# A two-layer hybrid block on one core: set-up work moved at the turns of the stages, and the second layer's projections cut to the tokens that the output needs

## The reference, cut to what matters

```python
h = concatenate([meta, x], 1)                      # 528 tokens
h = h + ssd_retention_mixer(rmsnorm(h, g0), ...)   # layer 0
h = h + conv_ffn(rmsnorm(h, g1), ...)
h = h + sb_lru_mixer(rmsnorm(h, g2), ...)          # layer 1
h = h + conv_ffn(rmsnorm(h, g3), ...)
return rmsnorm(h, final_norm)[:, N_META:]          # N_META = 16

def conv_ffn(h, w_in, conv_w, conv_b, w_out):
    u = causal_dwconv(h @ w_in, conv_w, conv_b)    # 3 taps: a token and the two before it
    g, up = jnp.split(u, 2, -1)
    return (jax.nn.silu(g) * up) @ w_out

def sb_lru_mixer(h, ...):
    q, k, v, gate, xr = split_cols(h @ w_in, ...)
    y_sb = stick_breaking_attention(q, k, v)       # causal: queries see the keys before them
    y_lru = rg_lru(causal_dwconv(xr, ...), ...) * gelu(gate)   # a scan over the tokens
    return concatenate([y_sb, y_lru], -1) @ w_out
```

## Time and profile before

| | |
|---|---|
| median of 3 runs | 1885.35 us (1885.19 to 1885.55) |
| profiled execution | 1886.69 us |
| its span, first to last instruction | 1884.7 us |
| PE busy | 1825.9 us, 97% of the span |
| DVE busy | 1221.8 us, 65% |
| ACT busy | 755.5 us, 40% |
| POOL busy | 68.5 us, 4% |
| mean granted TensorE clock | 0.994 |

### The profile page before, as it was taken

The page is one execution under the profiler, slowest core; times in us unless marked ns, Lnnn a source line. Parts: engine busy times, 40 slices in busy tenths (PEclk is TensorE's granted clock), DMA queues, the critical chain, the costliest instruction groups (busy, mean ns, idle before and its releaser), DMA issues.

```text
span 1884.7 us, 36044 instructions
## 1 busy us (share of the span) xinstructions
PE 1825.9 (97%) x14286; PEld 1737.0 (92%) x14286; DVE 1221.8 (65%) x1740; ACT 755.5 (40%) x1135; POOL 68.5 (4%) x140
## 2 busy tenths in 40 slices
PE   7999999999999999999999999999899999999996
PEld 7999998999899999999998888888789999999996
DVE  7787756455456777774334777777775688878323
ACT  5444432121234222222224777777774422223221
POOL 0122220000000000000000000000000000000000
PEclk9999999999999999999999999999999999999998
DMA  4222213222222222232222111111112222223221
GB/s 150 91 80 79 90 49 111 68 68 67 68 71 86 89 89 89 89 97 95 90 78 72 58 59 49 59 58 59 57 45 79 89 89 89 89 89 102 93 92 60
DMA packets 39938, 149.92 MB, mean 80 GB/s; under 512 B 4384, under 2 KB 5408, under 8 KB 39216
## 3 DMA queue, kind: packets, MB, share of 16 engines
q1 hardware_dynamic: 38672, 142.16, 24.1%
q10 hardware_dynamic: 1184, 6.60, 1.0%
HBM read 146.62 MB, written 2.13 MB: 79 GB/s over the span
## 4 chain that ended last, share of the span: by engine, by line
PE 71%; issue 12%; DVE 9%; ACT 6%; POOL 2%; DMA 0%; DVEq 0%; ACTq 0%; POOLq 0%
PE gp L359 60%; PE small L403 3%; PE small L414 3%; DVE spb L1502 1%; DVE sp_lo L1524 1%; ACT lbuf L922 1%; DVE wlo L1059 1%; ACT lbuf L925 1%; PE small L576 1%; POOL dec L1664 1%; PE small L553 1%; ACT whi L661 1%; PE small L561 1%; ACT L927 1%; ACT L995 0%
## 5 line engine op out<-in xcount | busy, mean ns | idle before, releaser
L359 PE MATMUL gp<-hn_hi,whi 128*128 128x264 f32 x3216 | 664.6, 288 | 23.0 <-DVE wlo L1059 12.2
L359 PE MATMUL gp<-hn_hi,wlo 128*128 128x264 f32 x3216 | 657.4, 286 | 0.0
L359 PE MATMUL gp<-hn_lo,whi 128*128 128x264 f32 x3216 | 656.7, 286 | 0.0
L661 ACT ACTIVATE whi<-raw 128x1024 fp32r<-128x1024 f32 (+1 forms) x249 | 273.6, 1099 | 775.5 <-PE gp L359 774.5
L1059 DVE TENSOR_TENSOR wlo<-raw,whi 128x1024 fp32r<-128x1024 f32 (+1 forms) x249 | 317.5, 1275 | 390.1 <-ACT whi L661 389.6
L359 PEld LDWEIGHTS gp<-hn_hi,whi 128*128 128x128 f32 x3216 | 503.0, 189 | 29.2 <-DVE wlo L1059 14.2
L359 PEld LDWEIGHTS gp<-hn_hi,wlo 128*128 128x128 f32 x3216 | 500.7, 189 | 0.0
L359 PEld LDWEIGHTS gp<-hn_lo,whi 128*128 128x128 f32 x3216 | 500.3, 189 | 0.0
L359 PE MATMUL gp<-hid_hi,whi 128*128 128x264 f32 x704 | 142.6, 284 | 0.0
L359 PE MATMUL gp<-hid_lo,whi 128*128 128x264 f32 x704 | 142.5, 284 | 0.0
L359 PE MATMUL gp<-hid_hi,wlo 128*128 128x264 f32 x704 | 142.5, 283 | 0.0
(11 more groups left out here) (241 smaller groups left out, 1907.1 us busy)
## 6 DMA issues: line engine op xcount, KB each, us to landing
raw<-in SPq DMA_DIRECT2D x217, 512.0 KB, 3.6
raw<-in SPq DMA_DIRECT2D x32, 704.0 KB, 4.1
cs_bc<-cs_scratch ACTq DMA_DIRECT2D x4, 1056.0 KB, 6.2
hT<-in SPq DMA_DIRECT2D x4, 528.0 KB, 7.4
out<-yT SPq DMA_DIRECT2D x4, 512.0 KB, 2.8
rdec<-in ACTq DMA_DIRECT2D x1, 1056.0 KB, 8.9
gw<-in SPq DMA_DIRECT2D x8, 128.0 KB, 3.4
rope<-in ACTq DMA_DIRECT2D x1, 528.0 KB, 5.8
```

The costliest lines, as they stand in the source:

```text
L359: ins = pe.matmul(gp[t.par][:, h, 0:H2], wp[w.par][:, cols], rp[:, k0 + k, h * H2:(h + 1) * H2], start=first and k == 0 and n == 0, stop=l ...
L661: act.activation(whi[w.par][:, 0:kt * P], raw[w.par][:, 0:kt * P], ACT.Copy).then_inc(hi_done, 1)
```

## The change

In layer 1, queries and gates, the output projection and the feed-forward's first product are computed for tokens 12 and on (t0 = FROM_MIX1), the convolution and hidden state for 14 and on, the feed-forward's second product for 16 and on. Halves are of 258 and 256 tokens then. Keys, values and xr stay whole. `gemm`, `evacuate`, `conv` and `add_tile` take a first token t0; each unit keeps its number of matmuls. The first 12 columns of qs and gt are set to zero once.

At the turns: the sum of squares goes behind k tile 3; the late `y_part` has its weight split behind k == 5 in place of 3, with the evacuation of tile 7 just ahead of that split; the first rotation of the queries goes behind split_lo and tile 7; hb and nsp (with ACT's three operations) are prepared at the start of the kernel; the memsets ahead of layer 1 go to GpSimd (POOL), behind `nlo_done` = 24, and DVE waits for them (`zero_done`) ahead of the first attention block.

```diff
+FROM_MIX1, FROM_CONV1, FROM_OUT = 12, 14, N_META
@@ gemm
-                            ins = pe.matmul(gp[t.par][:, h, 0:H2], wp[w.par][:, cols],
-                                            rp[:, k0 + k, h * H2:(h + 1) * H2],
+                            ins = pe.matmul(gp[t.par][:, h, 0:half], wp[w.par][:, cols],
+                                            rp[:, k0 + k, t0 + h * half:t0 + (h + 1) * half],
@@ norm_behind
-                return lambda k: sum_squares(n) if k == 1 else None
+                return lambda k: sum_squares(n) if k == 3 else None
@@ TensorE, layer 1
+            def l1_from(c):
+                return FROM_MIX1 if c in (0, 3) else 0
-                hgemm(At(0, 0, W_OUT1 + c), At(0, 0, T_OUT1 + c), after=after)
+                hgemm(At(0, 0, W_OUT1 + c), At(0, 0, T_OUT1 + c), after=after, t0=FROM_MIX1)
-            project(W_OUT1 + KD, T_OUT1 + KD, y_hi, y_lo, KD, (ylo_done, 3 * KD), per=1)
-            ffn_in(W_FI1, T_FI1, 3)
-            project(W_FO1, T_FO1, hid_hi, hid_lo, KH, (hlo_done, KF))
+            project(W_OUT1 + KD, T_OUT1 + KD, y_hi, y_lo, KD, (ylo_done, 3 * KD), per=1, t0=FROM_MIX1)
+            ffn_in(W_FI1, T_FI1, 3, t0=FROM_MIX1)
+            project(W_FO1, T_FO1, hid_hi, hid_lo, KH, (hlo_done, KF), t0=FROM_OUT)
@@ ScalarE, start
+            ch.link(act.activation(nspt[:], pcol("lru_lam", 0, 8), ACT.Abs))
             act.wait_ge(dtx_done, 1)
             ch.link(act.activation(dtl, dtx, ACT.Abs))
+            act.activation(nspt[:], nspt[:], ACT.Exp, scale=-1.0)
             ch.link(act.activation(dtl, dtl, ACT.Exp, scale=-1.0))
             act.activation(dtl, dtl, ACT.Ln, bias=1.0).then_inc(dtl_done, 1)
+            act.activation(nspt[:], nspt[:], ACT.Ln, bias=1.0).then_inc(spl_ln, 1)
@@ ScalarE, y_part (both late halves with split_at=5)
-                    if k == 3:
+                    if k == split_at:
                         split_hi(At(0, 0, wb + 1))
@@ ScalarE, into layer 1
             act.wait_ge(spl_done, 1)
-            ch.link(act.activation(nspt[:], pcol("lru_lam", 0, 8), ACT.Abs))
-            ch.link(act.activation(nspt[:], nspt[:], ACT.Exp, scale=-1.0))
-            act.activation(nspt[:], nspt[:], ACT.Ln, bias=1.0).then_inc(spl_ln, 1)
-            act.wait_ge(spl_done, 2)
@@ VectorE, start (behind the scan of csr)
+                    ve.tensor_scalar(hb[:, 0, :], pcol("lru_ba", 0, 8), 0.5, None, ALU.mult)
+                    ve.tensor_scalar(hb[:, 1, :], pcol("lru_bx", 0, 8), 0.5, None, ALU.mult)
+                    ch.link(ve.tensor_scalar(nsp[:], pcol("lru_lam", 0, 8), -1.0, 0.0, ALU.mult, ALU.max))
+                    ve.wait_ge(spl_ln, 1)
+                    ch.link(ve.tensor_tensor(nsp[:], nsp[:], nspt[:], ALU.add))
+                    ve.tensor_scalar(nsp[:], nsp[:], -0.5 * LRU_C, None, ALU.mult).then_inc(spl_done, 1)
@@ VectorE, retention
                         ret_tile(r - 1, 7)
                         if isinstance(r, int) and r == 1:
+                            rotate(0, rq, qr, 1, ch.link)
                             ve.wait_ge(rot_done, 1)
                             rotate(0, rk, kr, 3, ch.link)
...
             ve.wait_ge(tab_in, 32)
-            rotate(0, rq, qr, 1, ch.link)
             ret_stage(1)
@@ VectorE, y_part
-                    if k == 3:
+                    if k == split_at:
+                        if between is not None:
+                            between()
                         split_lo(At(0, 0, wb + 1))
...
-            add_tile(At(0, 0, W_OUT0 + 7), At(0, 0, T_OUT0 + 7), 7)
-            y_part(y_hi, y_lo, LATE[0], W_OUT0 + KD, KD)
+            y_part(y_hi, y_lo, LATE[0], W_OUT0 + KD, KD, 5, lambda: add_tile(At(0, 0, W_OUT0 + 7), At(0, 0, T_OUT0 + 7), 7))
@@ VectorE, layer 1 (the memsets and the preparation behind invert(2) are gone)
+                t0 = FROM_MIX1 if c in (0, 3) else 0
+                evacuate(w, t, halves(dst, t0), SB_SCALE if c == 0 else None, t0=t0)
...
+            ve.wait_ge(zero_done, 1)
             for b in range(2):
                 l1_block(0, b)
@@ GpSimd, behind the retention stage
+            po.wait_ge(nlo_done, 3 * KD)
+            for s in range(2):
+                po.memset(qs[s][:, 0:FROM_MIX1], 0.0)
+            po.memset(gt[:, 0:FROM_MIX1], 0.0)
+            po.memset(ubx[:, 0:3], 0.0)
+            for gap in (slice(WJ[1], LATER1), slice(LATER1 + WJ[2], LATER2), slice(LATER2 + WJ[3], LATER3)):
+                po.memset(later[:, gap], 0.0)
+            po.memset(spb[:, FULL:CAUSAL], 0.0)
+            po.memset(sp_lo[:, FULL:CAUSAL].bitcast(f32), 0.0)
+            po.memset(sp_hi[:, FULL:CAUSAL].bitcast(f32), 0.0).then_inc(zero_done, 1)
```

More of the change, by code:

```diff
@@ L150, in build @@
         eps_col = sb("eps_col", [P, 1])
+        hb = sb("hb", [P, 2, 8])
+        nsp, nspt = sb("nsp", [P, 8]), sb("nspt", [P, 8])
         idle_g, idle_v, idle_a = (sb(n, [P, 6]) for n in ("idle_g", "idle_v", "idle_a"))
@@ L231, in build, with halves, gout @@
         sp_ = ctx.enter_context(nc.psum_tensor("small", [P, 4, 512], f32))
[L233 to L237, removed]
+        def halves(ap, t0=0):
+            return ap[:, t0:T].rearrange("p (h t) -> p h t", h=2)
+        def gout(s, t0=0):
+            return gp[s][:, :, 0:(T - t0) // 2]
         def pcol(name, c=0, n=1, rows=P):
@@ L282, in build @@
             sem(n) for n in ("sum_done", "sphi_done", "later_done", "lathi_done", "latlo_done"))
-        prep_done, spl_done, spl_ln = sem("prep_done"), sem("spl_done"), sem("spl_ln")
+        prep_done, spl_done, spl_ln, zero_done = sem("prep_done"), sem("spl_done"), sem("spl_ln"), sem("zero_done")
         block = ctx.enter_context(nc.Block())
@@ L347, in _, with gemm @@
         def _(pe):
-            def gemm(w, t, rhs_hi, rhs_lo, k0=0, kt=KD, first=True, last=True, ready=None, after=None):
+            def gemm(w, t, rhs_hi, rhs_lo, k0=0, kt=KD, first=True, last=True, ready=None, after=None, t0=0):
+                half = (T - t0) // 2
                 pe.wait_ge(lo_done, w.v + 1)
@@ L366, in gemm, with hgemm @@
                         after(k)
-            def hgemm(w, t, ready=None, after=None):
-                gemm(w, t, hn_hi, hn_lo, ready=ready, after=after)
+            def hgemm(w, t, ready=None, after=None, t0=0):
+                gemm(w, t, hn_hi, hn_lo, ready=ready, after=after, t0=t0)
             def sum_squares(n):
@@ L504, in _, with project @@
                 ret_small(RET_HEADS - 1, c)
-            def project(wb, tb, rhs_hi, rhs_lo, kt, ready, per=2):
+            def project(wb, tb, rhs_hi, rhs_lo, kt, ready, per=2, t0=0):
                 def tile(i, s, first_pair):
@@ L510, in tile @@
                         gemm(At(2 * per, i, wb + per * s + kh), At(2, i, tb + s), rhs_hi, rhs_lo, k0=kh * kt, kt=kt,
-                             first=kh == 0, last=kh == per - 1, ready=ready if first_pair and s == 0 else None)
+                             first=kh == 0, last=kh == per - 1, ready=ready if first_pair and s == 0 else None,
+                             t0=t0)
                 for s in range(2):
@@ L627, in l1_block @@
                     hgemm(At(10, i, W_L1 + 5 * (b + 1) + c), At(10, i, T_L1 + 5 * (b + 1) + c),
-                          ready=ready if c == 0 else None, after=after)
+                          ready=ready if c == 0 else None, after=after,
+                          t0=FROM_MIX1 if ready is not None else l1_from(c))
             for c in range(5):
                 hgemm(At(10, 0, W_L1 + c), At(10, 0, T_L1 + c), ready=(nlo_done, 2 * KD) if c == 0 else None,
-                      after=norm_behind(2) if c == 0 else None)
+                      after=norm_behind(2) if c == 0 else None, t0=l1_from(c))
             for b in range(2):
@@ L1375, in _, with y_part @@
             ch.leave(2, RET_HEADS)
-            def y_part(dst_hi, dst_lo, tiles, wb, count):
+            def y_part(dst_hi, dst_lo, tiles, wb, count, split_at=3, between=None):
                 for k, y in enumerate(tiles):
@@ L1422, in ffn_in @@
             def ffn_in(wb, tb, L):
+                t0 = FROM_MIX1 * L
+                kept = slice(FROM_CONV1 * L, T)
                 def f_conv(i, half, dst, done):
@@ L1427, in f_conv @@
                     wait_count(ve, (cg_done, cu_done)[half], KF * L + i)
-                    evacuate(At(2, i, wb + half), t, halves(ubf[half][:, 2:2 + T]))
+                    evacuate(At(2, i, wb + half), t, halves(ubf[half][:, 2:2 + T], t0), t0=t0)
                     ve.wait_ge(pair_free[t.par], t.half + 1)
@@ L1477, in _ @@
             invert(2)
[L1480 to L1487, removed]
-            ve.tensor_scalar(nsp[:], pcol("lru_lam", 0, 8), -1.0, 0.0, ALU.mult, ALU.max).then_inc(spl_done, 1)
-            ve.wait_ge(spl_ln, 1)
-            ve.wait_ge(spl_done, 1)
-            ch.link(ve.tensor_tensor(nsp[:], nsp[:], nspt[:], ALU.add))
-            ve.tensor_scalar(nsp[:], nsp[:], -0.5 * LRU_C, None, ALU.mult).then_inc(spl_done, 1)
             def soft(n, e):
```

(8 more changed lines are left out.)

54 lines of the change are left out of this document (26 added, 28 removed).

## The result

The changed kernel takes 1863.99 us (median of 4 runs, 1863.77 to 1866.95) against 1885.27 us of before in the same session. The ratio is 0.9886, 95% interval 0.9871 to 0.9900: 21.3 us less, by the interval 19 to 24. The forecast was 1861.5 us. The profiled execution took 1863.77 us, its span is 1862.0 us, 22.7 us less than before's.

A forecast was written before the change was run, and what follows sets the result against it. TensorE (PE) was taken as the bound, by its matmul pace and pauses. Turns 13.1 us and columns 10.6 us, 23.7 off the 1885.35 us median, gave 1861.6, say 1861.5 us; range 1857.5 to 1872.5.

The forecast's parts named there:

- The turns: Pauses of PE between stages, moved work removing them and the low clock into layer 1: 13.1 us less in all.
- the columns: Layer 1's matmuls cut from 264 to 258 or 256 columns, at 0.417 ns a column: 10.6 us less.
- Turns 1 to 4: Retention 1.4 us; late output projections 2.3 and 2.4; sums of squares 2.9; into layer 1 2.6, plus 1.5 for clock.
- The deadline argument: Into layer 1: weight split done by 990.1, PE finishing unit 1 at 990.9, so no stall, 0.8 us to spare.
- The rotation's 1.4 us: Into retention: with the first query rotation behind weight split and tile 7, PE does not wait; 1.4 us gained.
- the low clock: Behind the pause into layer 1: 3.4 us at half clock, whose 15.5 matmuls cost 1.5 us that come back.
- Turn 5: Moved nsp and hb preparation (to the start) and memsets (to POOL) cost nothing; either hides.
- Rival A: Weight loads floor the matmul pace: columns give 0 to 5 us, turns all; 1867 to 1872.2 us, 20%.
- The 0.13 ns a column: Slope from the skill's spacings, 81 ns at 128 columns and 131 at 512; columns would give 3 us, not 10.
- Attention: Layer 1's attention stage keeps 0.6 of 1.9 us from shorter units; the rest only lengthens waits.
- rival C: Low clock at the pause of 1351.6 shortens from 6.8 to 3.4 us: 1.7 us less, 1859.8 us, 15%.
- Rivals B, D and E: Stall at layer 1's turn, 1865.6 us, 7%; slower shifted column starts, 1898, 2%; turn edits doing nothing, 1874.8, 3%.

## Why the prediction was right, and where it was off

**The total** is nearer than its terms. The turns gave 1.2 us more than forecast and the columns 2.2 us less (8.4 for 10.6), so the span's gain, 22.7 for 23.7, owes some of its closeness to luck.

**The bound** was read rightly: PE's matmuls and its pauses. What came off either came off the end.

**Turns 1 to 4** went by their steps: 14.3 us by unit starts for 13.1 forecast, each 0 to 0.4 us above. A pause costs a little more than idle + 0.16, since the first matmuls behind one start further apart (at 477.08 in the changed kernel the first two take 0.33 us, the next two 0.24). The deadline argument held: "0.8 us to spare" was 1.1. Two of the terms are less firm than written. The rotation's 1.4 us rested on a table that landed 8.9 us after its issue, which I took for a property of the kernel; with 6.2 us, as in one of the kernels above, it is nothing, and that it came out is partly luck. And the low clock was priced at 3.4 us as the trace of before had it; the same turn with its pause back had 6.8.

**Turn 5** right: nothing waits for what was moved, and POOL's memsets, bounded between 0.7 us and half of 22, take 0.8 in all.

**Columns**, the step that was mis-sized: "0.417: 2.5 ns at 258, 3.3 at 256". At 256 it is 3.3 against before's 121.36 ns, and 3.1 against the 121.11 that the same 264 columns take in the kernel with the turns alone, so the close match is partly luck. At 258 it is 1.5 against before's 121.67 (2.2 against the 122.36 of the kernel with the turns alone), because columns are paid in groups of four and 258 from column 12 or 270 touch 65 groups, as 260 would. That took 2.1 us from the feed-forward's first product and 0.4 from the late half, more than the whole miss of the span. The slope was worked out from 288, 416 and 264 columns, all multiples of four, and I carried it to a number that is not one. **Rival A**, a floor under the pace, exists, but at 111.7 ns: below about 240 columns, not here. That the weight loads make it is argued and not shown; the 64-column matmuls of the earlier trace rows even run at 106. The Trainium skill ("TensorE: Matmul & The Clock Gate", LDWEIGHTS) gives the time of a load of 128 columns as 128/1.2, an estimate of 107 ns, 5 less than the floor measured. The 0.13 ns a column that the prediction worked out, as an estimate, from two figures of the Trainium skill (same page, Back-to-back issue gap) does not hold here: between 240 and 264 columns of the feed-forward's second product the runs show 0.38.

**Attention**: 0.6 us forecast, 0.5 us when undone, each from one execution.

**From span to median**: the forecast took the span's 23.7 us off a median that lay 1.3 us below before's profiled execution, where the changed kernel's lies 0.2 above its own. The span's gain was 22.7, the median's 21.3 in one session and 23.4 in another. What the profiled executions differ by is mostly low clock: rival C was the right subject and too small a case. It is not only the length behind the known pause but whole further stretches in the attention stage, 2.8 to 2.9 us each.

**Rivals B, D and E** are out: no pause for wlo; no cost of a start at 12 (118.33 ns at 256 columns against 118.03 from 16) and at 270 none beyond the group of four; and the turns gave what they should.

## What to carry to other kernels

Cut the moving columns of a matmul at multiples of four (16 bytes of fp32), not in equal halves, and look for the floor (here 111.7 ns) before cutting further. At a turn, list for each engine what stands ahead of the next stage's first two weight splits and move it; price a pause with the low clock behind it. A term that rests on when one DMA landed in one execution is a range, not a number.

## What the runs showed of the hardware

- Matmuls of rounded fp32 with a weight load each, in units of 66, start 121.36, 118.03, 112.27 and 111.67 ns apart at 264, 256, 240 and 192 columns: 0.42 ns a column between the first two, 0.36 between the next, 0.01 at the end.
- The same loop of 48-matmul units with 264 columns keeps one of two paces through a whole stage, 121.67 or 122.36 ns. Layer 0's feed-forward had 122.36 in most kernels and 121.67 in two; layer 1's had 121.67 before the change and 122.36 with the turns alone. The units of 66 have 121.36 or 121.11. What chooses is open; it is worth 1.4 us in a feed-forward's first product.
- The granted clock fell to 1.2 GHz at every pause of PE of 2.5 to 6.2 us between stages, for 3.4, 6.8 or 10.2 us. The stretch began between 4.3 us before the pause's end and 0.3 us behind it, so the length alone does not price it: 3.1 to 6.0 us of it lay behind the pause.
- In six of the thirteen traces the clock fell once in the attention stage too, for 6.8 us, among small matmuls. Each time this was 2.3 to 2.4 us behind the pause of 0.9 us ahead of `v_out`, PE's longest there; which of the four such pauses, and whether any, differs between executions. In streams of whole units without a pause it never fell.
- A DMA of 1056 KB landed 6.1 to 9.4 us after its issue in kernels that hardly differ around it, and 6.4 and 7.7 us in two executions of the same one.
